# Attention projections fed before the norm is known: input parts split tile by tile, the norm's row factor applied on VectorE where results leave their banks

## The reference

```
def rmsnorm(x, gain):
    y = x * rsqrt(mean(x * x, axis=-1) + 1e-6)
    return y * gain

x = x + swiglu(rmsnorm(x, norm_ffn[0]), ffn_w_gate_up[0], ffn_w_down[0])   # layer 0 ends
h = rmsnorm(x, norm_mix[1])                                                # layer 1 begins
q, k, v, qi, ki, wi = split(h @ dsa_w_in)        # 1024, 1024, 1024, 512, 64 and 8 columns
q  = rope(rmsnorm(q per head, q_gain)); k = rope(rmsnorm(k per head, k_gain))
qi = rope(qi);                           ki = rope(rmsnorm(ki, None))
score = sum over index heads of relu(qi . ki) * wi          # per query and key, then causal
sel   = the 128 keys of highest score for each query
out   = softmax(q . k over sel) v;   x = x + out @ dsa_w_o
x = x + swiglu(rmsnorm(x, norm_ffn[1]), ...)                # last dense layer
```

## Time and profile before

| | us |
|---|---|
| median of three runs (3130.96 to 3171.21) | 3134.01 |
| the profiled execution | 3138.67 |
| its span in the profile | 3136.8 |
| stretch from the end of `down07` to the end of `pr0` | 23.6 |
| a key step, a query step of the loop (by TensorE) | 7.2, 8.8 |

### The profile page before, as it was taken

The page is one execution under the profiler, slowest core; times in us unless marked ns, Lnnn a source line. Parts: engine busy times, 40 slices in busy tenths (PEclk is TensorE's granted clock), DMA queues, the critical chain, the costliest instruction groups (busy, mean ns, idle before and its releaser), DMA issues.

```text
span 3136.8 us, 35702 instructions
## 1 busy us (share of the span) xinstructions
PE 2889.9 (92%) x12758; PEld 2233.8 (71%) x12758; DVE 1919.5 (61%) x2278; ACT 1400.3 (45%) x1794; POOL 244.2 (8%) x188
## 2 busy tenths in 40 slices
PE   7999999985999999999996579999989999999998
PEld 1547888764677777777774458888766767788877
DVE  3335654563888888888887674544335785454432
ACT  2323233223677777877775423333123425433321
POOL 1200100001950000000001000000011100000000
PEclk8999989995999999999998779999999999999999
DMA  6921722313799999989895702222221110022221
GB/s 228 328 90 48 276 96 92 122 54 148 282 353 362 365 372 364 381 355 386 351 386 189 88 33 94 94 94 94 94 76 67 68 68 1 28 94 94 94 94 67
DMA packets 90801, 546.92 MB, mean 174 GB/s; under 512 B 9232, under 2 KB 18848, under 8 KB 32384
## 3 DMA queue, kind: packets, MB, share of 16 engines
q1 hardware_dynamic: 79584, 485.65, 41.7%
q0 software_dynamic: 10816, 59.58, 5.5%
q10 hardware_dynamic: 288, 0.15, 0.0%
HBM read 516.51 MB, written 41.42 MB: 178 GB/s over the span
## 4 chain that ended last, share of the span: by engine, by line
PE 72%; DVE 16%; issue 6%; ACT 3%; DMA 3%; POOL 0%; SPq 0%; DVEq 0%; ACTq 0%; POOLq 0%; PEldq 0%
PE bank L348 40%; PE bank L286 6%; PE bank L1152 5%; PE bank L1156 4%; PE bank L1155 4%; DVE expert_low L2244 4%; DMA arena<-in_we_stream 2%; PE bank L1384 1%; PE bank L1406 1%; ACT expert_high L1601 1%; PE bank L1397 1%; PE bank L1136 1%; DVE arena L2346 1%; DVE expert_x_low L2329 1%; DVE arena L2594 1%
## 5 line engine op out<-in xcount | busy, mean ns | idle before, releaser
L2244 DVE TENSOR_TENSOR expert_low<-arena,expert_high 128x2048 fp32r<-128x2048 f32 x291 | 683.6, 2380 | 102.9 <-ACT expert_high L1601 84.5
L1601 ACT ACTIVATE expert_high<-arena 128x1024 fp32r<-128x1024 f32 x582 | 596.5, 1057 | 213.3 <-PE bank L1152 115.8
L721 DVE TENSOR_TENSOR weight_parts<-ring_pages,weight_parts 128x1024 fp32r<-128x1024 f32 x185 | 227.0, 1227 | 468.7 <-ACT weight_parts L713 468.2
L713 ACT ACTIVATE weight_parts<-ring_pages 128x1024 fp32r<-128x1024 f32 x185 | 196.1, 1060 | 456.3 <-PE bank L348 413.2
L348 PE MATMUL bank<-high_b,weight_parts 128*128 128x512 f32 x1168 | 371.3, 399 | 13.8 <-DVE low_p L2482 7.8
L348 PE MATMUL bank<-low_b,weight_parts 128*128 128x512 f32 x1056 | 354.2, 389 | 0.0
L1152 PE MATMUL bank<-expert_high,expert_x_low 128*128 128x512 f32 x768 | 309.2, 403 | 14.7 <-DVE expert_low L2244 11.0
L1155 PE MATMUL bank<-expert_high,expert_x_high 128*128 128x512 f32 x768 | 300.9, 392 | 0.0
L1156 PE MATMUL bank<-expert_low,expert_x_high 128*128 128x512 f32 x768 | 300.3, 391 | 0.0
L348 PEld LDWEIGHTS bank<-high_b,weight_parts 128*128 128x128 f32 x1168 | 219.9, 189 | 72.4 <-issue 20.9
L348 PEld LDWEIGHTS bank<-low_b,weight_parts 128*128 128x128 f32 x1056 | 198.2, 188 | 41.9 <-issue 0.5
(11 more groups left out here) (476 smaller groups left out, 4500.8 us busy)
## 6 DMA issues: line engine op xcount, KB each, us to landing
arena<-in_we_stream SPq DMA_DIRECT2D x294, 1024.0 KB, 6.7
ring_pages<-in_wb_stream SPq DMA_DIRECT2D x93, 1024.0 KB, 4.8
ring_pages<-in_wa_stream SPq DMA_DIRECT2D x49, 1024.0 KB, 4.9
arena<-in_mod POOLq DMA_DIRECT2D x16, 1024.0 KB, 5.2
xbuf<-arena POOLq DMA_DIRECT2D x25, 512.0 KB, 16.0
arena<-xbuf SPq DMA_DIRECT2D x17, 512.0 KB, 7.4
ybuf<-arena SPq DMA_DIRECT2D x16, 512.0 KB, 2.6
arena<-kd SPq DMA_DIRECT2D x8, 512.0 KB, 22.4
```

The costliest lines, as they stand in the source:

```text
L713: nc.scalar.activation(high, src, ACT.Copy).then_inc(weights_high, 1)
L721: nc.vector.tensor_tensor(low, src, high.bitcast(F32), ALU.subtract).then_inc(weights_split, 1)
L1601: nc.scalar.activation(ehigh[c % HIGH_E][:, at], ring_e[c % RING_E][:, at], ACT.Copy) \
L2244: nc.vector.tensor_tensor(elow[c % RING_E][:], ring_e[c % RING_E], ehigh[c % HIGH_E][:].bitcast(F32), ALU.subtract).then_inc(weights_split ...
```

## The change

The norm's factor of a token can be taken out of a product: (x * gain * RS) W = (x * gain) W * RS. The changed kernel uses this for `pr{s}` and `dv`, as both kernels do for the dense layers.

- The parts of `x * gain` are made tile by tile under the down projections of the first dense layer: `input_tile` (ScalarE: high part, then square) and `input_low` (VectorE). `normed_all`, `raw` and `high_part` go.
- `sn3` moves from ahead of `pr0` to behind it, and with it TensorE's wait for the rotation tables. The weights of `pr1` are split ahead of the root.
- VectorE takes `pr{s}` out of its bank, multiplied by `RS`, in all 21 steps. ScalarE then squares the tile that VectorE wrote (17 steps), and multiplies query tiles by their gain in place. The root of block s-1 keeps its place behind this square.
- `dv` leaves its banks on ScalarE with a scale per token, for which `RS` is turned by four small transposes beside those of `wi` in step 6; `wi` is multiplied by it.
- Tiles change pages (`qT`, `low_b` for `low_p`, the squares, the late hidden tiles), and the square of tile 5 to 7 waits for a sum of GpSimd that frees its place.

```diff
-JOBS_B += [f"gu0{b}" for b in range(1, 2 * FFT)] + [f"down0{j}" for j in range(KT)] + ["sn3"]
+JOBS_B += [f"gu0{b}" for b in range(1, 2 * FFT)] + [f"down0{j}" for j in range(KT)]
-        JOBS_B += [f"pr{_s}"] + [f"ix{t}{i}" for t, i in indexed_at(_s)]
+        JOBS_B += [f"pr{_s}"] + (["sn3"] if _s == 0 else []) + [f"ix{t}{i}" for t, i in indexed_at(_s)]
...
-            squares(3)
-            pe.wait_ge(S["b_rope_in"], 48)
             for s in range(NR + 2):
                 if s < NR:
-                    by_columns(f"pr{s}", (ROPED[s][0], ROPED[s][1]), lambda kt: (high_b[:, kt, :], low_p[:, kt, :]),
+                    by_columns(f"pr{s}", (ROPED[s][0], ROPED[s][1]), lambda kt: (high_b[:, kt, :], low_b[:, kt, :]),
                                split_before=None if s else 2 * KT + FFT)
+                    if s == 0:
+                        squares(3)
+                        pe.wait_ge(S["b_rope_in"], 48)
...
+                            ins = pe.transpose(ps[:, (NTX + t) * IH:(NTX + t + 1) * IH], RS[0:IH, t * P:(t + 1) * P],
+                                               ident[0:IH, 0:IH])
...
+            def input_tile(n, kt):
                 act.wait_ge(S["b_x_ready"], KT * (n - 2) + kt + 1)
+                name, first = gain_in[n]
+                nc.scalar.activation(parts_in[n][0][:, kt, :], x[:, kt, :], ACT.Copy, scale=col(name, first + kt)) \
                     .then_inc(high_ready, 1)
+                if n == 3 and kt >= 5:
+                    act.wait_ge(S["sq_summed"], sums_made(n, kt - 4))
+                nc.scalar.activation(square_at(n, kt), x[:, kt, :], ACT.Square).then_inc(S["b_sq_full"], 1)
...
                 for j in range(KT):
                     weights_high_part(act, ahead(f"down{n}", f"down{n}", j, FFT), split_to)
+                    if n == 0 and j:
+                        input_tile(3, j - 1)
...
-            for kt in range(KT):
-                squared_tile(3, kt)
+            input_tile(3, KT - 1)
+            weights_high_part(act, half_of("dqi", 0) + 1, split_to)
+            nc.scalar.activation(wi_parts[:, 0], wiw[:], ACT.Copy).then_inc(S["small_operands"], 1)
             rooted(3)
-
-            high_part(high_b, raw, S["b_h_full"], h_count[3] - KT)
...
-                        copied(act, nc.scalar.activation(vt[:, t, n * 512:(n + 1) * 512], ps[:], ACT.Copy),
-                               S["b_v_rows"], n_row, f"dv{n}{t}")
+                        copied(act, nc.scalar.activation(vt[:, t, n * 512:(n + 1) * 512], ps[:], ACT.Copy,
+                                                         scale=rs_rows[:, t:t + 1]), S["b_v_rows"], n_row, f"dv{n}{t}")
                 if s < NR:
-                    ps = result(act, f"pr{s}")
                     if ROPED[s][2]:
+                        act.wait_ge(S["b_rs_scaled"], s + 1)
                         k = norm_index[s]
                         if k >= 2:
                             act.wait_ge(bank_done, JB[f"pn{norm_of[k - 2]}"] + 1)
-                        nc.scalar.activation(sqt[:, k % 2, :], ps[:], ACT.Square).then_inc(S["b_sqt_ready"], 1)
-                    gain = col("qk_gain", 0) if ROPED[s][2] == "rows" else 1.0
-                    copied(act, nc.scalar.activation(roped_tile(s), ps[:], ACT.Copy, scale=gain), S["b_raw_ready"], s + 1,
-                           f"pr{s}")
+                        nc.scalar.activation(sqt[:, k % 2, :], roped_tile(s), ACT.Square).then_inc(S["b_sqt_ready"], 1)
+                        act.wait_ge(S["b_sqt_ready"], k + 1)
+                    if ROPED[s][2] == "rows":
+                        nc.scalar.activation(roped_tile(s), roped_tile(s), ACT.Copy, scale=col("qk_gain", 0)) \
+                            .then_inc(S["b_raw_ready"], 1)
...
+                    if n == 0 and j:
+                        input_low(3, j - 1)
...
-            normed_all(3, "norm_mix", KT, low_p)
-            dve.wait_ge(S["b_rope_in"], 48)
+            input_low(3, KT - 1)
+            weights_low_part(dve, half_of("dqi", 0) + 1, split_to)
...
+            rms(3)
+            dve.wait_ge(S["b_rope_in"], 48)
...
+                if s < NR:
+                    copied(dve, nc.vector.tensor_tensor(roped_tile(s), result(dve, f"pr{s}")[:], RS[:], ALU.mult),
+                           S["b_rs_scaled"], s + 1, f"pr{s}")
                 if 1 <= s <= NR and ROPED[s - 1][2] == "tile":
...
-                    dve.wait_ge(S["b_raw_ready"], s)
...
+                    link(nc.vector.tensor_copy(rs_rows[:], by_head(1)[:, :, 0]))
+                    link(nc.vector.tensor_scalar(wi, by_head(0), float(IH) ** -0.5, float(HD) ** -0.5, ALU.mult, ALU.mult))
+                    link(nc.vector.tensor_tensor(wi, wi, rs_rows[:].unsqueeze(2).to_broadcast([P, NTX, IH]), ALU.mult))
```

More of the change, by code:

```diff
@@ L613, in block_kernel, with square_at, sums_made @@
         hb = page(12, KT, T)
-        sqb = {n: page(first, KT, T) for n, first in ((2, 24), (3, 16), (4, 24))}
+        sqb = {n: page(first, slots, T) for n, first, slots in ((2, 24, KT), (3, 42, 5), (4, 24, KT))}
+        def square_at(n, kt):
+            return sqb[n][:, kt if n != 3 or kt < 5 else 1 + (kt - 1) % 4, :]
+        def sums_made(n, k):
+            return 2 + (KT - 1) * (n - 2) + k
         u2 = page(16, S5G, S5C)
@@ L644, in hid @@
             if n:
[L645 to L646 removed]
+                i, k = (0, kt) if kt < 9 else (1, kt - 9) if kt < 14 else (2, kt - 14)
+                return hid_late[i][:, k, 0, :], hid_late[i][:, k, 1, :]
             half = hid_parts[kt // (FFT // 2)]
             return half[:, 0, kt % (FFT // 2), :], half[:, 1, kt % (FFT // 2), :]
[L650 to L654 removed]
+        parts_in = {2: (high_b, low_b), 3: (high_b, low_b), 4: (low_p, high_g)}
+        gain_in = {2: ("norm_ffn", 0), 3: ("norm_mix", KT), 4: ("norm_ffn", KT)}
+        qT, kT = page(38, KT, T), page(20, KT, T)
         vt = page(24, NTX, D)
@@ L1307, in dense @@
             def dense(n):
-                high, low = ffn_in[n]
+                high, low = parts_in[2 + 2 * n]
                 for b in range(2 * FFT):
@@ L1335, in _ @@
                         for kt in range(KT):
-                            for w, h in ((0, low_p), (0, high_b), (1, high_b)):
+                            for w, h in ((0, low_b), (0, high_b), (1, high_b)):
                                 ins = pe.matmul(ps[0:IH, :], wi_parts[:, w, kt, :], h[:, kt, :],
-                                                start=(kt == 0 and h is low_p), stop=(kt == KT - 1 and w == 1))
+                                                start=(kt == 0 and h is low_b), stop=(kt == KT - 1 and w == 1))
                         ins.then_inc(bank_done, 1)
@@ L2490, in _, with input_low @@
             n_sig, n_x, n_hid = 0, 0, 0
-            def ffn_low(n, kt):
+            def input_low(n, kt):
                 n_high[0] += 1
                 dve.wait_ge(high_ready, n_high[0])
-                high, low = ffn_in[n]
-                nc.vector.scalar_tensor_tensor(out=low[:, kt, :], in0=x[:, kt, :], scalar=col("norm_ffn", KT * n + kt),
+                high, low = parts_in[n]
+                name, first = gain_in[n]
+                nc.vector.scalar_tensor_tensor(out=low[:, kt, :], in0=x[:, kt, :], scalar=col(name, first + kt),
                                                in1=high[:, kt, :].bitcast(F32), op0=ALU.mult, op1=ALU.subtract) \
@@ L2512, in _ @@
                 if j:
-                    ffn_low(0, j - 1)
-            ffn_low(0, KT - 1)
+                    input_low(2, j - 1)
+            input_low(2, KT - 1)
             n_x = KT
-            def normed_all(n, gain, first, low):
-                rms(n)
-                for kt in range(KT + 1):
-                    if kt < KT:
-                        normed(raw, kt, col(gain, first + kt), S["b_h_full"], h_count[n] - KT + kt + 1)
-                    if kt:
-                        low_tile(low, high_b, raw, kt - 1)
             def dense_dve(n, n_sig, n_x):
```

63 lines of the change are left out of this document (21 added, 42 removed).

## The result

The changed kernel took 3203.54 us (median of 4 executions, 3195.45 to 3241.45), the kernel before beside it 3134.08. The ratio is 1.0217, 95% interval 1.0156 to 1.0279: slower by 69 us, but whether by more than two per cent the interval leaves open. The prediction, 3155 in a range of 3127 to 3178, had the sign and missed the size. The profiled execution took 3195.48 us, its span is 3193.7, against 3138.67 and 3136.8 before: +56.9 us between the two profiles.

What follows compares the result with a forecast made beforehand. It took TensorE to bind up to about step 19 and VectorE's queue from there. The terms -21.9, +17.9 and +24.9 gave +20.9 us on the median of 3134.0, so 3155 us, range 3127 to 3178.

Steps and rivals of the forecast that it cites:

- the gap: From the first dense layer's last down projection through `pr2`: serial norm hidden under TensorE's work, -21.9 us.
- sum (E - M): Total shift carried into the attention: -21.9 + 17.9 + 24.9 = +20.9 us.
- +3 us: At the gap: allowance if the rotation tables meet a 1 MB weight load and land later.
- The key steps: Projection steps 5 to 13: a loop over VectorE and ScalarE takes 9.38 us against 7.22, in sum +17.9 us.
- The query steps: Projection steps 14 to 20: the same loop, longer, takes 11.0 us for TensorE's 8.8, in sum +24.9 us.
- Behind it: From step 20's weight part on: VectorE never pauses, so the shift enters the attention whole, with nothing added.
- C: Projection steps: TensorE's pauses lower its granted clock, about +35 us more, 3190; chance 4%.
- A: Projection steps: the multiply fills VectorE's idle time, TensorE keeps its pace, -22 us, 3112; chance 10%.
- the sum by it: Whole change by occupancy ranking: 14 us of VectorE work moved under TensorE's cover, -21.9 us.

Runs made afterwards that it cites:

- the work alone: Kernel before with one more VectorE multiply, its result unread, in each of the 21 steps; 3132.4, 3189.4, 3195.4 and 3218.3 us.
- six fills in the attention: Kernel before with six more matmuls, results unread, in attention steps 34 to 39; 3132.4 to 3149.8 us, ratio 0.9967.
- square last: Changed kernel with ScalarE's square and gain copy moved behind relus, root and weight part in each step; median 3129.2 us, ratio 0.9958.
- square last with sixteen fills: Changed kernel with ScalarE's square and gain last, plus unread matmuls in attention steps 0 to 9 and 34 to 39; ratio 1.002.
- shifts of 1 and 3 us: Changed kernel with one more VectorE reciprocal, half or full width, ahead of the dense layers; ratios 1.0249 and 1.0266.

## Why the prediction missed

Point by point, as it was worked out, each counted from M so that the scatter ahead of the boundary drops out:

| | forecast | measured |
|---|---|---|
| the gap (M to the end of `pr2`) | -21.9 | -18.2 |
| to the reciprocal of step 13 | +17.9 | +17.7 |
| from there to the end of step 20's weight part | +24.9 | +22.1 |
| from there to E | 0 | 0.0 |
| sum (E - M) | +20.9 | +21.6 |

The reciprocal of step 13 in the chain of waits after, for the second and third line:

```profile
2453.70 3.36 DVE arena L2605
```

- *The gap.* The tables landed 9.4 us behind M, forecast 7.4: the last took 5.3 us from issue to landing, not 3.1. That is the "+3 us" of the prediction. Behind TensorE's wait for them, 3.9 us, `pr1` and `pr2` took 12.80 us and not twice 5.5, with a granted clock of 0.54 from 2337.6 to 2341.1.
- *The key steps*, a loop of 9.38 us over six pieces: measured 9.39. The mechanism holds, with the named waits, and was shown by taking it apart (the work alone cost 4.5 us, the root ahead of the square gives back 14.0). That the sum is right to 0.01 us is luck. The hand-overs and ScalarE's wait on itself took 0.03 to 0.04 us each where 0.10 and 0.17 were put in, 0.26 too much with the square. VectorE's own part took 0.27 more than forecast: the rotation's add is 1.09 us in that step where the row had 0.69, and VectorE's wait on itself 0.04 for 0.17.
- *The query steps*, 11.0 us: measured 9.7, 9.7, 10.7 and 10.3 from multiply to multiply in those without picks, 14.4 and 15.4 with picks. They came out 2.8 us under the forecast in all.
- *The sum* up to the attention, +20.9 for +21.6, owes its closeness to the gap and the query steps missing by 3.7 and 2.8 us in opposite directions.
- *Behind it: "the shift is carried whole into the attention"* and nothing else changes. **This step failed.** Had it held, the profiled execution would have been 2597.2 + 558.6 + 1.9 = 3157.7 us, and 3155 would have been right. In its place the granted clock fell to 0.50 for 85 us, +37.9 us in the profile. In the profile of another execution, of 3242.8 us, it was at 0.50 in two places, 2602 to 2732 and 2742 to 2807. None of 18 executions of the changed kernel, 8 of them shifted, held the clock; of the kernel before 51 of 91 did.

The clock had been a rival (*C*, 4%), but looked for in the projection steps. There it stayed at 1.00 in most steps (2404.6 to 2414.0 and 2502 to 2513) and was low in a few short stretches:

```profile
2420.00:2424.00 4.00, 4.00 (x13) 3.13 (x12) 2.40 (x4) 1.81 (x3) 0.68 (x1) 0.60 0.80 262
...
2524.00:2528.00 4.00, 1.34 (x2) 0.00 (x0) 3.67 (x4) 0.00 (x0) 1.26 (x1) 0.50 0.43 98
2528.00:2532.00 4.00, 0.00 (x0) 0.00 (x0) 3.76 (x10) 0.00 (x0) 0.00 (x0) 0.50 0.39 164
```

In the last two TensorE mostly waits (busy 1.34 of 8), and the loop as a whole came out under its forecast, so nothing of the miss lies there. The rival's price of +35 stood at the wrong place, and that its 3190 is near the profile's 3195 is chance. The rows to see it were at hand: the three times of the kernel before reach from 3130.96 to 3171.21, a spread of 40 us that the prediction took as scatter of 0.3%. Of its executions beside the experiments those up to 3139 have a mean clock of 0.955 to 0.960 and those from 3158 on one of 0.949 and under, and six fills in the attention left none above 3150. No execution of the upper group of the kernel before was profiled, so that its clock falls in the attention too is inferred from this. A kernel whose own executions divide between 3135 and 3172 has a stage on the edge, and an edit ahead of that stage can decide on which side it comes down.

Rival *A*, that VectorE's work just fits into TensorE's step, would have failed also with the loop gone: with square last the key step is 8.11 us, not 7.20. The sum of six durations left out what lies between them, and the rotation's add took 0.86 and 1.09 us in these steps where the row had 0.69. The Trainium skill (Perfetto Trace Analysis, section Identifying the Most-Contended Engine) advises to rank engines by occupancy, and the prediction put the sum by it at -21.9. The runs do not bear that sum out: E - M moved by -17.2 with the multiply left out, and by +21.6 with it in the chain.

**What stays open** is what in the changed kernel sets the fall off. Shown is that it is the clock, where it falls, and what it costs. Excluded as sufficient causes are the attention's instructions and pages, and a pause of TensorE; its place in time only as far as shifts of 1 and 3 us go. A late start of the attention is not needed: the clock fell in a profile of square last with sixteen fills, whose E is 2563.4. A rival that the runs leave standing is the length of the stretch ahead of the attention. The share that held goes from 7 of 10 (E - M 238.2) over 51 of 91 (248.3) and 4 of 10 (255.9) to 0 of 18 (269.9 and more), but 0 of 10 at 258.4 and 4 of 10 at 257.0 do not line up, and the fills change the share at the same length. Not tried: shifts of more than 3 us, fills at other places than the ten, and the changed loop with its wait ahead of `dv` filled with matmuls. The version with the square last has the lowest median of all (3129.2, ratio 0.9958), but by its interval it is not faster than the kernel before.

## What to carry to other kernels

- An added instruction is priced by the chain in which it stands: 14.5 us of VectorE work cost 4.5 us beside the chain and 38.7 us in it. Where two in-order engines hand a value back and forth, add up the whole circle, hand-overs and waits on itself included, and look for an order in which one of them comes to the value late (here square and gain last).
- Read the spread of the times of the kernel before as a row. Two groups 35 us apart say that a stage loses its clock in some executions; then price every edit ahead of it with that loss, and compare by groups or at a mark ahead of the stage, not by medians.
- Take the difference of two marks, one on each side of the edit. One mark alone moved by up to 13 us between profiles of the same code, and made an edit of +4.5 us look like -1.3 and one of +10.0 like -2.9.

## What the runs showed of the hardware

- At the lower level of the clock the attention's small matmuls (64 to 512 columns) keep TensorE busy 84.92 of 85 us, and the clock did not rise for 85 us here, and for 130 us (2602 to 2732, busy 129.0) in a second profile of the same kernel.
- In one stage the fall began at two places: in the first steps, or some 75 us later, at 2672, shortly behind an idle time of TensorE of 1.11 us that ended at 2670.25. The kernel before has the same 1.11 us of idle time, up to 2653.93, and held its clock at 1.00, so that this idle time alone does not set the fall off. The first line is the changed kernel's, the second that of the kernel before.

```profile
2670.25 0.46 PE L1419 MATMUL bank<-arena 64*128 64x128 f32 x2 [1.11 <-DVEq L770]
```

```profile
2653.93 0.46 PE L1406 MATMUL bank<-arena 64*128 64x128 f32 x2 [1.11 <-DVEq L764]
```

- A hand-over between ScalarE and VectorE took 0.10 us in the kernel before (root to reciprocal at 2396.59) and 0.03 us in the loop of the changed kernel (2411.89 + 0.69 to 2412.61, 2413.28 + 0.69 to 2414.00). ScalarE's square to its root took 0.04 us there, though ScalarE waits 0.17 us on itself in other places. They are not constants that can be carried from one step to another.
